# A two-block transformer on one core: the last expert pair adds into token-major PSUM, the final norm works per token tile, and the last eight weight chunks load in parts

## The chip, the core and the metric

The kernel runs on one core of one Trainium2 chip. A core has TensorE (matrix products, called PE in the rows; its weight loads are PEld), VectorE (DVE), ScalarE (ACT), GpSimd (POOL) and SyncE (SP), which issues most DMA transfers. The engines run their own instruction streams and meet at semaphores. Products land in PSUM, eight banks of 128 partitions x 512 float32; everything else lives in SBUF, in 128 partitions. The metric is the device time of one execution in microseconds (us). Lower is better.

## The reference, cut to what matters

Two transformer blocks on 512 tokens of width 1024, all in float32. Only the end of the second block is touched: the expert layer and the final norm.

```
D_MODEL = 1024; SEQ = 512; N_EXPERTS = 16; CAPACITY_FACTOR = 2; D_EXPERT = 2048

def rmsnorm(x, g):
    y = xf * lax.rsqrt(jnp.mean(xf * xf, axis=-1, keepdims=True) + EPS)
    return (y * g.astype(jnp.float32)).astype(x.dtype)

def expert_choice_ffn(h, w_router, w_gate, w_up, w_down):
    cap = max(1, CAPACITY_FACTOR * N // N_EXPERTS)            # 64
    aff = jax.nn.softmax(logits, axis=-1)
    top_w, top_idx = lax.top_k(jnp.swapaxes(aff, 1, 2), cap)
    xe = jax.vmap(lambda hb, ib: hb[ib])(h, top_idx)
    g = jnp.einsum('becd,edf->becf', xe, w_gate)
    u = jnp.einsum('becd,edf->becf', xe, w_up)
    y = jnp.einsum('becf,efd->becd', jax.nn.silu(g) * u, w_down)
    y = y * top_w[..., None].astype(y.dtype)
    return ...zeros((N, D)).at[ib.reshape(-1)].add(yb.reshape(-1, D))

    h2 = modulate_2(rmsnorm(x, norm2_g[l]), sh2, sc2)
    x = x + g2 * expert_choice_ffn(h2, ...)
    return rmsnorm(x, final_g)
```

Each of the 16 experts picks 64 tokens and multiplies them with three matrices of 8 MB each, 384 MB of weights in all.

## The kernel before

The first two thirds of the time (both blocks up to the router) are the same in both kernels. Then the experts follow in eight pairs, the loop `for it in range(PAIRS)` on every engine. The two experts of a pair share the 128 rows of the array: one takes PSUM partitions 0 to 63, the other 64 to 127.

A pair needs 24 weight chunks of 2 MB (`load`, L731): eight of the gate matrix, eight of up, eight of down. Each is [128 x 4096] float32, so a partition gets one run of 16 KB. There are eight chunk buffers (`eslots`: six tensors called weights, two pieces of the tensor arena). SyncE issues the chunks in order, each as soon as TensorE has counted the buffer's last user free (`chunk_free`). TensorE takes the chunks two by two, one per expert; such a step j has 16 matmuls of 512 columns.

Within a pair, TensorE does four steps of gate into banks 0 to 3, four steps of up into banks 4 to 7 (`widen`, L1301 and L1303), turns the hidden rows (`turn_hidden`, L1334), gathers the next pair's tokens (L1284) and does four steps of down into banks 4 and 5 (L1364 and L1367). ScalarE applies Silu (L1872), copies the turned rows (L1876) and, when the last down chunk is done, copies the two banks of y to SBUF (L1882). The next pair's first step is followed by `scatter` (L1316): eight matmuls, one for each 128 features, multiply y with a 0/weight matrix and give the pair's contribution feature-major, [128 features x 512 tokens]. VectorE multiplies each by the column g2 and adds it to the residual xT (L2506). So the scatter of a pair lies beside the next pair's weight stream.

After the last pair nothing follows that could cover it. There the order is: the two copies of y, the eight scatter matmuls, the eight adds; ScalarE squares each of the eight feature tiles (L1397) and TensorE sums over the features with 32 matmuls of one column (`norm_step`, L824); root and reciprocal of the [128 x 4] sums; VectorE has multiplied xT by the final weight in the meantime (L2531); TensorE turns 32 blocks of 128 x 128 back to token-major (L811), ScalarE and VectorE multiply by the reciprocal (L1391, L2537) and SyncE stores four tiles of 512 KB (L750).

The PSUM banks of the shared tiles are given out in order by `plan_banks`; the expert loop uses banks by number.

Of the kernel before, what the change touches and what calls it, by code (L numbers as in the profile page):

```python
# [25 lines left out]
ALU = mybir.AluOpType  # L26
# [114 lines left out]
def plan_banks():  # L141
# [129 lines left out]
    b.add("nf2", "A")  # L271
    for t in range(TT):
        for hh in range(2):
            b.add(("ot", t, hh), "AD"[hh])
# [3 lines left out]
def build_two_blocks(nc, x, c, ctx, c_ctx, w_mod, b_mod, norm1_w, w_in, ret_decay_f, ret_decay_b,  # L278
# [8 lines left out]
    with es:  # L287
# [42 lines left out]
        def slot(i, k):  # L330
# [11 lines left out]
            f_ready stored decay_exp stage2_in mod_summed mod_landed0 mod_landed1 mod_landed2""".split()  # L342
# [190 lines left out]
        LAST_BANK = 0 if banks.bank("nf2") >= 4 else 4  # L533
# [9 lines left out]
        norm_tags = ["n1", "nc", "n2", "n3", "nf1", "nc2", "n4", "nf2"]  # L543
# [4 lines left out]
        NTH_SQUARES = {2: 0, 3: 1, 4: 2, 6: 3, 7: 4}  # L548
# [122 lines left out]
        out_sb = at(0, TT, D)  # L671
# [17 lines left out]
        def _(sp):  # L689
# [53 lines left out]
            for it in range(PAIRS):  # L743
                for m in range(ESLOTS if it == 0 else 0, PAIR_CHUNKS):
                    sp.wait_ge(S["chunk_free"], LOOP_FREE + it * PAIR_CHUNKS + m - ESLOTS + 1)
                    load(it, m)
            for t in range(TT):
                for hh in range(2):
                    wait_freed(sp, ("ot", t, hh))
                sp.dma_start(out[0, t * P:(t + 1) * P, :], out_sb[:, t, :]).then_inc(S["stored"], 16)  # L750
            sp.wait_ge(S["stored"], 16 * TT)
# [3 lines left out]
        def _(pe):  # L755
# [563 lines left out]
            def weigh(it):  # L1319

                pe.wait_ge(S["hmt_ready"], FQ * it + 2)
                for t in range(TT):
                    pe.matmul(bank(1)[:, 0:2], sels[it % 2][:, t, :], aff[:, t, 2 * it:2 * it + 2],
                              start=(t == 0), stop=(t == TT - 1))
                for e in range(2):
                    pe.matmul(bank(0)[64 * e:64 * e + 64, :],
# [3 lines left out]
            def turn_hidden(it, n):  # L1330

                pe.wait_ge(S["hm_ready"], FQ * it + n + 1)
                for r in range(4):
                    last = pe.transpose(bank(n)[:, r * P:(r + 1) * P],  # L1334
                                        hmid[:, n * 512 + r:(n + 1) * 512:4], ident)
                last.then_inc(S["hmt_full"], 1)

# [3 lines left out]
            for it in range(PAIRS):  # L1341
                if it:
                    pe.wait_ge(S["wsel_ready"], it)
                for j in range(STEPS):
# [3 lines left out]
                    elif j == 0:  # L1348
                        gather(0, range(2, STEPS))
                if it:  # L1350
                    pe.wait_ge(S["x_added"], KT * it)
                for j in range(STEPS):
                    widen(it, j, 2 * STEPS, S["up_full"])
                for n in range(FQ):
# [3 lines left out]
                for j in range(STEPS):  # L1358
                    pe.wait_ge(S["hmt_ready"], FQ * it + j + 1)
                    m = 4 * STEPS + 2 * j  # L1360
                    wa, wb = expert_chunk(it, m, 4), expert_chunk(it, m + 1, 4)
                    for r in range(4):
                        for hh in range(2):
# [10 lines left out]
            pe.wait_ge(S["wsel_ready"], PAIRS)  # L1374
            scatter(PAIRS - 1, LAST_BANK)
            for k in range(KT):
# [1372 lines left out]
```

## Time and profile before

| | |
|---|---|
| time, median of 3 runs | 2497.77 us (2495.11 to 2498.15) |
| time of the profiled execution | 2498.93 us |
| its span in the trace | 2496.7 us |
| mean granted TensorE clock | 0.971 |
| busy share of PE, DVE, ACT, POOL | 93%, 36%, 25%, 6% |
| HBM read | 566.35 MB, 228 GB/s over the span |

Times in the rows are counted from the start of the span; the profiled execution's own time is 2.2 us longer than its span. A matmul in float32 appears in the trace as two records where it is a product and as one where it is a transpose. "x16" is a number of records, and records that follow each other overlap, so the distance from one start to the next is the cost of one, not its length. The granted clock has two levels: 1.00 is 2.4 GHz and 0.50 is 1.2 GHz.

### The profile page before, as it was taken

Reading aid. Unit: us, or ns where it says so; the run is one execution under the profiler, and the core shown is the slowest. Engines: PE = TensorE matmul, PEld = TensorE weight load, DVE = VectorE, ACT = ScalarE, POOL = GpSimd, SP = SyncE. Lnnn points to the kernel's source line nnn. Section 1 sums busy time; section 2 is a strip of 40 time slices with the busy share of each in tenths; the row PEclk is TensorE's granted clock in tenths of the full one; section 3 lists DMA queues with packets and bytes.
Section 4 is the critical chain, followed back from the end, with each engine's and each line's share of the span. In section 5 each row is a group of like instructions: output and inputs, shape, how many; then the busy total and the mean of one; then the engine's idle time right before and its main releaser. Section 6 shows DMA issues by size and latency. Waiting matters only on the chain.

```text
span 2496.7 us, 25781 instructions
## 1 busy us (share of the span) xinstructions
PE 2324.9 (93%) x11168; PEld 1520.2 (61%) x11168; DVE 897.7 (36%) x1178; ACT 621.6 (25%) x876; POOL 146.5 (6%) x140
## 2 busy tenths in 40 slices
PE   6999999999999999998999997988998889898988
PEld 4874878877888878786677885434343434242434
DVE  4937445455688334545632433010000000010102
ACT  5314333243334235415533221000000000000001
POOL 0221000110000011210000020000000000000000
PEclk8999999999999999999999998999999999999998
DMA  7220444344554331210012235999999999999994
GB/s 269 101 79 1 151 160 142 122 149 169 187 183 171 136 135 68 82 65 32 1 35 101 72 131 239 423 428 428 428 427 428 427 428 427 428 427 428 428 428 171
DMA packets 111190, 570.10 MB, mean 228 GB/s; under 512 B 5390, under 2 KB 28215, under 8 KB 86503
## 3 DMA queue, kind: packets, MB, share of 16 engines
q1 hardware_dynamic: 95200, 523.57, 51.9%
q0 software_dynamic: 7152, 27.99, 3.2%
q10 hardware_dynamic: 8727, 16.91, 1.9%
q8 instruction: 88, 1.44, 0.2%
q14 instruction: 23, 0.19, 0.0%
HBM read 566.35 MB, written 2.10 MB: 228 GB/s over the span
## 4 chain that ended last, share of the span: by engine, by line
PE 73%; DMA 19%; DVE 4%; ACT 2%; issue 1%; ACTq 0%; SPq 0%; POOL 0%; DVEq 0%; POOLq 0%
PE ps L772 42%; DMA arena<-in_w_exp_up 9%; PE ps L1301 8%; PE ps L1364 6%; DMA arena<-in_w_exp_gate 6%; PE ps L1284 3%; DMA weights<-in_w_exp_gate 2%; PE ps L1187 1%; PE ps L1205 1%; DMA arena<-in_w_exp_down 1%; PE ps L1145 1%; DMA weights<-in_w_up 1%; PE ps L1011 1%; PE ps L1316 1%; PE ps L1164 1%
## 5 line engine op out<-in xcount | busy, mean ns | idle before, releaser
L772 PE MATMUL ps<-weights_r 128*128 128x512 f32 (+1 forms) x2784 | 860.2, 389 | 12.1 <-DVE hT_r L1929 4.0
L772 PEld LDWEIGHTS ps<-weights_r 128*128 128x128 f32 x2784 | 521.0, 189 | 125.2 <-issue 18.7
L772 PE MATMUL ps<-hT_r,weights_r 128*128 128x512 f32 x1264 | 462.6, 390 | 0.0
L1301 PE MATMUL ps<-weights,arena 128*64 128x512 f32 x768 | 355.2, 620 | 61.0 <-DMA weights<-in_w_exp_up 47.7
L1303 PE MATMUL ps<-weights,arena 128*64 128x512 f32 x768 | 355.9, 621 | 0.0
L1301 PEld LDWEIGHTS ps<-weights,arena 128*64 128x64 f32 x768 | 106.2, 142 | 290.6 <-issue 288.6
L1910 DVE TENSOR_TENSOR weights_r<-weights,weights_r 128x4096 fp32r<-128x4096 f32 (+1 forms) x46 | 197.1, 4284 | 209.2 <-ACT weights_r L1447 207.4
L772 PEld LDWEIGHTS ps<-hT_r,weights_r 128*128 128x128 f32 x1264 | 238.3, 188 | 51.0 <-issue 2.2
L772 PE MATMUL ps<-arena_r,weights_r 128*128 128x512 f32 (+1 forms) x640 | 225.1, 388 | 0.0
L1447 ACT ACTIVATE weights_r<-weights 128x4096 fp32r<-128x4096 f32 (+1 forms) x46 | 161.6, 3514 | 214.8 <-PE ps L772 118.9
L2521 DVE TENSOR_TENSOR hT<-hT,ps 128x512 f32<-128x512 f32 x32 | 22.0, 688 | 461.8 <-PE ps L1303 461.8
L1364 PE MATMUL ps<-weights,hT 128*64 128x512 f32 x384 | 168.4, 594 | 2.3 <-DMA weights<-in_w_exp_down 2.3
L1367 PE MATMUL ps<-weights,hT 128*64 128x512 f32 x384 | 168.4, 594 | 0.0
L1301 PE MATMUL ps<-arena 128*64 128x512 f32 x256 | 119.3, 621 | 25.1 <-DMA arena<-in_w_exp_up 17.3
L772 PEld LDWEIGHTS ps<-arena_r,weights_r 128*128 128x128 f32 x640 | 120.6, 189 | 24.3
L1303 PE MATMUL ps<-arena 128*64 128x512 f32 x256 | 119.6, 622 | 0.0
L1364 PEld LDWEIGHTS ps<-weights,hT 128*64 128x64 f32 x384 | 51.2, 137 | 109.8 <-issue 108.8
L2506 DVE SCALAR_TENSOR_TENSOR xT<-ps,mod_cols,xT 128x512 f32<-128x512 f32 x64 | 48.0, 751 | 184.7 <-PE ps L1316 178.7
L1303 PEld LDWEIGHTS ps<-weights,arena 128*64 128x64 f32 x768 | 106.2, 142 | 0.0
L1301 PEld LDWEIGHTS ps<-arena 128*64 128x64 f32 x256 | 35.6, 143 | 101.4 <-issue 101.3
L1876 ACT ACTIVATE hT<-ps 128x512 f32<-128x512 f32 x32 | 16.5, 599 | 311.1 <-PE ps L1334 311.1
L1872 ACT ACTIVATE hT<-ps 128x512 f32<-128x512 f32 x32 | 19.1, 597 | 278.5 <-PE ps L1303 278.5
(294 smaller groups left out, 2531.6 us busy)
## 6 DMA issues: line engine op xcount, KB each, us to landing
weights<-in_w_exp_gate SPq DMA_DIRECT2D x48, 2048.0 KB, 23.1
weights<-in_w_exp_up SPq DMA_DIRECT2D x48, 2048.0 KB, 27.0
weights<-in_w_exp_down SPq DMA_DIRECT2D x48, 2048.0 KB, 27.1
weights<-in_w_in SPq DMA_DIRECT2D x18, 2048.0 KB, 8.3
arena<-in_w_exp_gate SPq DMA_DIRECT2D x16, 2048.0 KB, 27.1
arena<-in_w_exp_up SPq DMA_DIRECT2D x16, 2048.0 KB, 28.3
arena<-in_w_exp_down SPq DMA_DIRECT2D x16, 2048.0 KB, 28.5
weights<-in_w_up SPq DMA_DIRECT2D x22, 1024.0 KB, 7.7
```

The costliest lines, as they stand in the source:

```text
L772: last = pe.matmul(t, a if w_first else b, b if w_first else a, start=(k == 0 and n == 0), stop=(k == kt - 1 and n == len(pairs) - 1))
L1011: last = pe.matmul(t, v1[:, i, (2 * j + g) * DV:(2 * j + g + 1) * DV], probs[j % 2][g][:, i, :], start=(start and i == 0), stop=(not start ...
L1145: local = pe.matmul(ps[:, c:c + w], q2[o:o + 64, 2 * kv + p, n * P:(n + 1) * P], kdup[o:o + 64, kv, b0 * P:b1 * P], start=True, stop=False)
L1164: last = pe.matmul(ps[:, c + w + k0:c + w + k1], q2[o:o + 64, 2 * kv + p, n * P:(n + 1) * P], kcdup[o:o + 64, kv, k0:k1], start=True, stop ...
L1284: last = pe.matmul(bank(6, 2)[:, d * P:(d + 1) * P], h2_tok[:, t, 256 * j + r:256 * j + 256:2], sels[it % 2][:, t, :], start=(t == 0), sto ...
L1301: la = pe.matmul(bank(b0 + n)[0:64, :], xe[:, 2 * j + r, 0:64], wa[:, r, n * 512:(n + 1) * 512], start=start, stop=stop)
L1303: lb = pe.matmul(bank(b0 + n)[64:128, :], xe[:, 2 * j + r, 64:128], wb[:, r, n * 512:(n + 1) * 512], start=start, stop=stop)
L1364: la = pe.matmul(bank(4 + hh)[0:64, :], hmid_t[:, 4 * j + r, 0:64], wa[:, r, hh * 512:(hh + 1) * 512], start=(j + r == 0), stop=(j == STEP ...
L1367: lb = pe.matmul(bank(4 + hh)[64:128, :], hmid_t[:, 4 * j + r, 64:128], wb[:, r, hh * 512:(hh + 1) * 512], start=(j + r == 0), stop=(j == ...
L1447: A(slots_r[high_slot(i)][:, 0:n], slots[sl][:, 0:n], ACT.Copy).then_inc(S["high_ready"], 1)
L1910: ve.tensor_tensor(slots_r[sl][:, 0:n], slots[sl][:, 0:n], slots_r[high_slot(i)][:, 0:n].bitcast(F32), ALU.subtract).then_inc(S["low_ready ...
L2506: ve.scalar_tensor_tensor(xT[:, d, :], ps[:, b * 512:(b + 1) * 512], mod_cols2[:, 40 + d, 0:1], xT[:, d, :], ALU.mult, ALU.add).then_inc(S ...
```

## The change

In the last pair alone, the result is built token-major. While the last pair's weights stream, TensorE puts the residual of each of the four token tiles into two PSUM banks by multiplying xT with the identity (`turn_rest`); the last scatter then adds onto it, with the selection matrix as the stationary operand and y as the moving one. Since g2 can't be a per-partition column there, two rows (g2 and the final weight, each repeated over 128 partitions) are made by TensorE (`spread_rows`) and kept by ScalarE; y is multiplied by the g2 row when it leaves PSUM. The norm then is one squaring with a running sum per tile, a root, a reciprocal, and one VectorE operation per half tile that multiplies by both the reciprocal and the final weight. The last eight chunks load in halves (down steps 0 to 2) or quarters (step 3), with a semaphore of their own for each later part, and the down matmuls wait part by part.

```diff
+        TOKEN_BANKS = (0, 2, 6, 4)
+        g2_row, final_row = at(0, D), at(D, D)
+        out_sb = slots[0][:, :].rearrange("p (t d) -> p t d", t=TT)
+        squared = slots[1][:, :].rearrange("p (t d) -> p t d", t=TT)
@@ SyncE
+            for j in range(STEPS):
+                sp.wait_ge(S["chunk_free"], LOOP_FREE + PAIRS * PAIR_CHUNKS - 2 * ESLOTS + 2 * j + 2)
+                n = 4 if j == STEPS - 1 else 2
+                for i in range(n):
+                    for e in range(2):
+                        sl, w = 2 * j + e, SLOT // n
+                        src = w_exp_down_2[0, NE - 2 + e, 512 * j:512 * j + 512, :].rearrange(
+                            "(p r) n -> p (r n)", r=4)
+                        done = S[f"last{i}"] if n == 4 else S[f"late{j}"] if i else S[f"landed{sl}"]
+                        sp.dma_start(eslots[sl][:, i * w:(i + 1) * w], src[:, i * w:(i + 1) * w]).then_inc(done, 16)
+            for t in range(TT - 1):
+                sp.wait_ge(S["out_ready"], 2 * t + 2)
                 sp.dma_start(out[0, t * P:(t + 1) * P, :], out_sb[:, t, :]).then_inc(S["stored"], 16)
+            for hh in range(2):
+                sp.wait_ge(S["out_ready"], 2 * TT - 1 + hh)
+                sp.dma_start(out[0, L - P:L, hh * 512:(hh + 1) * 512], ...
@@ TensorE
+            def spread_rows(it):
+                pe.wait_ge(S["x_added"], KT * it)
+                for i, src in enumerate((mod_cols2[:, 40:48, 0], cols[:, 3, V1["final"]:V1["final"] + KT])):
+                    for k in range(KT):
+                        last = pe.matmul(bank(4 + 2 * i, 2)[:, k * P:(k + 1) * P],
+                                         src[:, k:k + 1].broadcast_to([P, P]), ident, start=True, stop=True)
+                    last.then_inc(S["rows_full"], 1)
+            def turn_rest(t):
+                for k in range(KT):
+                    pe.matmul(bank(TOKEN_BANKS[t], 2)[:, k * P:(k + 1) * P], xT[:, k, t * P:(t + 1) * P], ident,
+                              start=(k % 4 == 0), stop=False)
...
+                    if j == 2 and it == PAIRS - 1:
+                        spread_rows(it)
...
+                    if it == PAIRS - 1 and j in (1, 2):
+                        pe.wait_ge(S["silu_done"], FQ * PAIRS)
+                        turn_rest(j - 1)
...
+                        if in_parts:
+                            pe.wait_ge(S[f"last{r}"], 32)
+                        elif it == PAIRS - 1 and r == 2:
+                            pe.wait_ge(S[f"late{j}"], 32)
...
+                    if it == PAIRS - 1 and j == 2:
+                        pe.wait_ge(S["wsel_ready"], PAIRS)
+                        turn_rest(2)
-            scatter(PAIRS - 1, LAST_BANK)
-            for k in range(KT):
-                norm_step(7, "nf2", L, k)
             for t in range(TT):
+                if t == TT - 1:
+                    turn_rest(t)
                 for hh in range(2):
-                    turn(("ot", t, hh), [(k * P, hT[:, 4 * hh + k, t * P:(t + 1) * P]) for k in range(4)])
+                    pe.wait_ge(S["yg_ready"], hh + 1 if t == 0 else 2)
+                    pe.matmul(bank(TOKEN_BANKS[t] + hh), wsel_ts[(PAIRS - 1) % 2][:, t * P:(t + 1) * P],
+                              y_sb[:, hh * 512:(hh + 1) * 512], start=False, stop=True).then_inc(S["tok_full"], 1)
@@ ScalarE
+            A(small[:, 4:5], eps_col, ACT.Sqrt)
             for t in range(TT):
+                act_e.wait_ge(S["tok_full"], 2 * t + 2)
+                A(squared[:, t, :], ps[:, b * 512:(b + 2) * 512], ACT.Square,
+                  accum_out=tok_sums[:, t:t + 1]).then_inc(S["tok_squared"], 1)
+                act_e.wait_ge(S["tok_squared"], t + 1)
+                A(root[:, t:t + 1], tok_sums[:, t:t + 1], ACT.Sqrt, bias=eps_col, scale=1.0 / D).then_inc(
+                    S["tok_root"], 1)
@@ VectorE
+            for hh in range(2):
+                ve.tensor_tensor(y_sb[:, hh * 512:(hh + 1) * 512], bank(4 + hh), g2_row[:, hh * 512:(hh + 1) * 512],
+                                 ALU.mult).then_inc(S["yg_ready"], 1)
+            for t in range(TT):
+                ve.wait_ge(S["tok_root"], t + 1)
+                ve.reciprocal(recip[:, t:t + 1], root[:, t:t + 1]).then_inc(S["tok_recip"], 1)
+                ve.wait_ge(S["tok_recip"], t + 1)
+                for hh in range(2):
+                    c = slice(hh * 512, (hh + 1) * 512)
+                    ve.scalar_tensor_tensor(out_sb[:, t, c], bank(TOKEN_BANKS[t] + hh), recip[:, t:t + 1],
+                                            final_row[:, c], ALU.mult, ALU.mult).then_inc(S["out_ready"], 1)
```

In the last pair the turned hidden rows go to banks 4 to 7 and the last weight selection (`weigh`) to banks 6 and 7, since banks 0 to 3 then hold residuals; `weigh` therefore waits for all four copies of the turned rows, and the first down step for two.

TensorE's stream after the last matmul pairs of the last down step, in the kernel before (ps is PSUM, arena and hT are SBUF tensors; L1364 and L1367 are down, L1316 the scatter, L824 the sums, L811 the turns back):

```order
L1364 MATMUL ps<-arena,hT 64x512
L1367 MATMUL ps<-arena,hT 64x512
L1316 MATMUL ps<-arena 128x512 x8
L824 MATMUL ps<-mean_ones,arena 128x1 x32
L811 MATMUL ps<-cst,hT 128x128 x32
L287 UNCONDITIONAL_BRANCH
```

The same place in the changed kernel, with the waits (L1416 and L1419 are down, L1434 the scatter, L1372 `turn_rest`):

```order
L1416 MATMUL ps<-arena,hT 64x512 [waits last3]
L1419 MATMUL ps<-arena,hT 64x512
L1434 MATMUL ps<-arena 128x512 [waits yg_ready] x6
L1372 MATMUL ps<-cst,xT 128x128 x8
L1434 MATMUL ps<-arena 128x512 [waits yg_ready] x2
L283 UNCONDITIONAL_BRANCH
```

The sums and the turns back are gone; eight matmuls with the identity stand between the sixth and the seventh scatter matmul. Three more groups of eight stand earlier in the last pair: after up steps 1 and 2, and between down steps 2 and 3.

ScalarE's stream from the turned hidden rows of the last pair on, in the kernel before:

```order
L1876 ACTIVATE hT<-ps 128x512 x4
L1882 ACTIVATE arena<-ps 128x512 x2
L1417 ACT_TABLE_LOAD
L1417 ACTIVATE small<-small 128x1
L1397 ACTIVATE arena<-xT 128x512 x8
L1391 ACTIVATE small<-ps,small 128x4
L1391 ACTIVATE arena<-ps,small 128x512 x4
```

And in the changed kernel, where the last two rows stand four times:

```order
L1936 ACTIVATE hT<-ps 128x512 x4
L1945 ACT_TABLE_LOAD
L1945 ACTIVATE small<-small 128x1
L1949 ACTIVATE weights,small<-ps 128x1024
L1952 ACTIVATE small<-small 128x1
```

The copies of y have moved to VectorE, the table load stands ahead of the wait for the first token tile, and one squaring reads 1024 columns of PSUM at once.

SyncE's stream of the last down chunks and the stores, before:

```order
L731 DMA weights<-in_w_exp_down 128x4096 x6
L731 DMA arena<-in_w_exp_down 128x4096 x2
L750 DMA out<-arena 128x1024 x4
```

And after:

```order
L764 DMA weights<-in_w_exp_down 128x2048 x12
L764 DMA arena<-in_w_exp_down 128x1024 x8
L767 DMA out<-weights 128x1024 x3
L770 DMA out<-weights 128x512 x2
```

Eight loads have become twenty, and four stores five.

## Rows read from the trace of the kernel before

**Rows 1.** The page's strip: what the DMA engines moved, in 40 equal slices.

```profile
GB/s 269 101 79 1 151 160 142 122 149 169 187 183 171 136 135 68 82 65 32 1 35 101 72 131 239 423 428 428 428 427 428 427 428 427 428 427 428 428 428 171
```

**Rows 2.** The chain of waits: start, length, what; its last 70 us.

```profile
2429.53 29.80 DMA arena<-in_w_exp_down
2459.46 1.08 PE ps L1364
...
2468.09 1.09 ACT arena L1882 x2
2469.32 7.11 PE ps L1316 x16
2476.42 10.49 PE ps L824 x64
2486.91 5.03 PE ps L811 x32
```

**Rows 3.** Windows: stretch, length, busy of five engines, granted clock, DMA share, GB/s.

```profile
14.00:16.00 2.00, 2.00 (x16) 2.00 (x15) 0.84 (x2) 1.99 (x4) 0.00 (x0) 1.00 1.05 385
...
2200.00:2220.00 20.00, 20.00 (x100) 7.39 (x100) 3.16 (x9) 0.00 (x0) 0.00 (x0) 1.00 1.01 428
...
2457.00:2458.00 1.00, 0.00 (x0) 0.00 (x0) 0.00 (x0) 0.00 (x0) 0.00 (x0) 1.00 0.12 49
...
2480.00:2490.00 10.00, 10.00 (x49) 10.00 (x49) 1.30 (x3) 1.34 (x3) 0.00 (x0) 0.51 0.00 0
```

**Rows 4.** TensorE's timeline in the last pair; in brackets the idle time before.

```profile
2410.57 0.61 PE L1301 MATMUL ps<-weights,arena 128*64 128x512 f32 x1 [1.01 <-DMA weights<-in_w_exp_up]
...
2420.38 0.61 PE L1301 MATMUL ps<-arena 128*64 128x512 f32 x1 [2.71 <-DMA arena<-in_w_exp_up]
...
2431.22 0.64 PE L1364 MATMUL ps<-weights,hT 128*64 128x512 f32 x1
...
2439.94 0.61 PE L1364 MATMUL ps<-weights,hT 128*64 128x512 f32 x1 [1.63 <-DMA weights<-in_w_exp_down]
...
2446.96 1.05 PE L1323 MATMUL ps<-arena 128*128 128x2 f32 x8
...
2449.73 0.61 PE L1364 MATMUL ps<-weights,hT 128*64 128x512 f32 x1 [0.71 <-DMA weights<-in_w_exp_down]
...
2459.46 1.08 PE L1364 MATMUL ps<-arena,hT 128*64 128x512 f32 x1 [2.65 <-DMA arena<-in_w_exp_down]
...
2467.41 0.59 PE L1364 MATMUL ps<-arena,hT 128*64 128x512 f32 x1
```

**Rows 5.** The chain again: the last gather, 32 matmuls of 128 columns.

```profile
2312.28 7.54 PE ps L1284 x64
```

**Rows 6.** Groups by form on ScalarE and VectorE: busy, mean ns, idle before.

```profile
L1404 ACT ACTIVATE arena<-weights 128x1024 f32<-128x1024 f32 x8 | 8.4, 1048 | 0.0
L1404 ACT ACTIVATION_READ_ACCUMULATOR arena<-weights 128x1 f32 x8 | 1.5, 190 | 0.0
...
L2521 DVE TENSOR_TENSOR hT<-hT,ps 128x512 f32<-128x512 f32 x32 | 22.0, 688 | 461.8 <-PE ps L1303 461.8
```

**Rows 7.** ScalarE's and VectorE's timeline at the very end.

```profile
2469.19 1.28 ACT L1417 ACT_TABLE_LOAD   x1
...
2487.01 0.26 ACT L1391 ACTIVATE small<-ps,small 128x4 f32<-128x4 f32 x1 [9.13 <-PE ps L824]
...
2487.30 0.18 DVE L2534 RECIPROCAL small<-small 128x4 f32<-128x4 f32 x1 [6.93 <-ACT small L1391]
...
2490.21 2.50 DVE L2537 TENSOR_SCALAR arena<-ps,small 128x512 f32<-128x512 f32 x3 [0.64 <-PE ps L811]
```

**Rows 8.** DMA issues: count, KB of each, median us to landing.

```profile
weights<-in_w_in SPq DMA_DIRECT2D x18, 2048.0 KB, 8.3
...
out<-arena SPq DMA_DIRECT2D x4, 512.0 KB, 2.9
```

More of the change, by code:

```diff
@@ L670, in build_two_blocks, with turned_at, weighed_at @@
         hmid_t = hT[:, 4:8, :].rearrange("p a b -> p (a b)").rearrange("p (k n) -> p k n", k=16)
-        out_sb = at(0, TT, D)
+        def turned_at(it):
+            return 4 if it == PAIRS - 1 else 0
+        def weighed_at(it):
+            return 6 if it == PAIRS - 1 else 0
+        g2_row, final_row = at(0, D), at(D, D)
+        out_sb = slots[0][:, :].rearrange("p (t d) -> p t d", t=TT)
+        squared = slots[1][:, :].rearrange("p (t d) -> p t d", t=TT)
+        tok_sums = small[:, 48:52]
         decay = small[:, 8:24]
@@ L1358, in _ @@
                 for j in range(STEPS):
-                    pe.wait_ge(S["hmt_ready"], FQ * it + j + 1)
+                    pe.wait_ge(S["hmt_ready"], FQ * it + (max(j + 1, 2) if it == PAIRS - 1 else j + 1))
                     m = 4 * STEPS + 2 * j
-                    wa, wb = expert_chunk(it, m, 4), expert_chunk(it, m + 1, 4)
+                    in_parts = it == PAIRS - 1 and j == STEPS - 1
+                    if in_parts:
+                        wa, wb = (eslots[ESLOTS - 2 + e][:, :].rearrange("p (r n) -> p r n", r=4) for e in range(2))
+                    else:
+                        wa, wb = expert_chunk(it, m, 4), expert_chunk(it, m + 1, 4)
                     for r in range(4):
+                        if in_parts:
+                            pe.wait_ge(S[f"last{r}"], 32)
+                        elif it == PAIRS - 1 and r == 2:
+                            pe.wait_ge(S[f"late{j}"], 32)
                         for hh in range(2):
@@ L1866, in _ @@
                 free_before = LOOP_FREE + it * PAIR_CHUNKS
+                if it == PAIRS - 1:
+                    for i, dst in enumerate((g2_row, final_row)):
+                        act_e.wait_ge(S["rows_full"], i + 1)
+                        for hh in range(2):
+                            A(dst[:, hh * 512:(hh + 1) * 512], ps[:, (4 + 2 * i + hh) * 512:(5 + 2 * i + hh) * 512],
+                              ACT.Copy).then_inc(S["rows_kept"], 1)
                 for n in range(FQ):
```

70 lines of the change are left out of this document (29 added, 41 removed).

## The prediction, made before the changed kernel ran

> **What bounds the kernel now.** I read the page's strip first. From its 26th slice on the DMA engines move 427 or 428 GB/s in every slice, until the last, half empty one [rows 1]: the expert stage is bound by its weight stream. A matmul pair hidden or saved before the stream's end therefore buys nothing; what counts is what follows the last byte. The chain of waits says what that is [rows 2]. The last down chunk, issued at 2429.5, lands at 2459.4, and TensorE starts on it at 2459.46. From there to the end of the span, 2496.7, there are 37.2 us without a weight load: the last down step to 2468.0 (8.5 us), two copies of y to 2469.2, the scatter to 2476.4, the sums of squares to 2486.9, the turns back to 2491.9, then the last scaling and store. A single window, 2457 to 2458, shows the stream running out, at 49 GB/s [rows 3]: a few of the 16 engines end later than the others, and a chunk waits for the latest.
>
> In TensorE's timeline the reader is to see the waits in front of the steps [rows 4]. Up and down steps start 9.8 us apart (2410.57 to 2420.38, 2439.94 to 2449.73) since their 4.19 MB take that long; the work of a step, 16 pairs of records, is 6.9 us: `weigh` starts 7.0 us behind the step's first record (2439.94 to 2446.96), so a quarter of it is 1.72 and a pair 0.43. After an idle time of 1.63 us or less the first record lasts 0.61 to 0.64 us; the last down step, after 2.65 us of idle time, opens with 1.08 us, the lower clock level (1.2 GHz).
>
> **The change, part by part: up to the end of down.** The new matmuls with the identity, `turn_rest`, are products of 128 columns like the gather's, 32 of which took 7.54 us [rows 5]: 0.236 each, 1.9 us for a group of eight. `spread_rows` has 16, 3.8 us, in the gate phase. There and in up the 2.9 us between a step's work and the next landing cover them; the loads wait for chunks that are freed up to 2.5 us later, but the last of them has 29.8 us from issue to landing [rows 2], so the stream doesn't run dry. The first two groups even help: the group after up step 1 ends at about 2411.5 instead of the start at 2410.57, so step 2 ends near 2418.4, the second group near 2420.3, and step 3 starts at its landing, 2420.38, without the 2.71 us of idle time and without the low clock after it. That takes some 1.7 us off, and down starts at 2429.5 instead of 2431.22 [rows 4]. The wait for a second copy of turned rows costs nothing, since that copy is 0.5 us behind the first and TensorE still turns the last two.
>
> Then down, with halves landing 4.9 us ahead of the whole. Step 0 ends at 2436.4. The first half of step 1 is there at about 2435.2, the second at 2440.0; its two halves of work (3.4 us each) end at 2439.8 and, with a wait of 0.4, at 2443.7. `weigh` takes 2.0 us (2446.96 to 2449.0 before) to 2445.7. Step 2: first half at once, to 2449.1; the second lands at about 2450.3; done at 2453.7. The third group: 2455.6. Step 3 then has its first quarters already there and works through four times 1.72 us, to 2462.5. The other bound is the last quarter: landing at 2459.4 plus what the cutting costs (0.9, below), plus 1.72, is 2462.1. I take 2462.5, against 2468.0 before: a gain of 5.5 us, of which most is the parts' and the rest the higher clock.
>
> What cutting costs is not shown for 8 KB and 4 KB runs. The nearest rows bound it: at full DMA share 2 KB runs moved 385 GB/s and 16 KB runs 428 [rows 3]. One sixteenth of each, per packet, is 85.1 and 612.5 ns; a straight line through both has about 10 ns for a packet beside its bytes. The eight chunks have 1,024 packets of 16 KB; in parts they have 1,536 of 8 KB and 1,024 of 4 KB, which is 96 more for each engine, 0.9 us. The ends are 0 and the 2 KB rate for all 16.8 MB: 43.6 instead of 39.2 us, 4.4 us.
>
> The Trainium skill (DMA: Bandwidth & Descriptors, Why small descriptors are slow) gives a packet a fixed overhead of about three bus cycles. By its 850 MHz that would be an estimated 3.5 ns, 0.3 us in all; the row of the 2 KB runs speaks for more, and the sum goes by the row.
>
> **From the end of down to the end.** Before: 2468.0 to 2496.7, 28.7 us. Now: VectorE's product with the g2 row, PSUM to SBUF, 0.69 us [rows 6] and 0.07 for the semaphore; 0.15 to TensorE's start, as between 2469.17 and 2469.32 [rows 2]. The eight scatter matmuls cost what the old ones did, 7.11 / 8 = 0.89 each, 7.1 us; the fourth group, which stands between them, 1.9; 0.15 for the last to drain. TensorE ends 10.1 us after down. The second product of VectorE (0.69) lies beside the first matmul. The waits added here have behind them only the remaining matmuls of the same kind.
>
> For each token tile ScalarE squares 1024 columns with a sum, 1.05 + 0.19 [rows 6], and takes a root, 0.2; the reciprocal is 0.18 and two operations with the row are 0.83 apart [rows 7], 1.6 together. TensorE delivers a tile each 1.8 us, ScalarE needs 1.5 and VectorE 1.9 for one, and the fourth tile comes 3.7 us after the third. So three tiles lie beside TensorE's work and only the last one counts: 0.05 + 1.24 + 0.3 (root with its two hops) + 0.23 + 0.1 + 1.6 = 3.5 us. The table load (1.28 us, rows 7) now stands before the first wait, beside the down steps, at no cost; if that cover were gone it would cost nothing either way for the last tile. That root and squares need no further load is in the order of before, where eight squares and a root follow one load.
>
> The store: before, the last operation of VectorE ends at 2492.71 [rows 7] and the span at 2496.7, 4.0 us with four stores of 512 KB close together. Now the last is 256 KB and nearly alone. Its ends are 2.3 (the 2.9 of a 512 KB store [rows 8] less 0.6 for half the bytes) and 4.0; I take 3.3.
>
> The sum: 10.1 + 3.5 + 3.3 = 16.9 us instead of 28.7, a gain of 11.8. With the 5.5 that makes 17.3: span 2479.4. The profiled execution took 2498.93, so its like would take 2481.6; it lies 1.2 above the median of the runs shown. From 2497.77 the median comes to 2480.5.
>
> **The rivals.** *The stream ends later.* If parts move at the rate of 2 KB runs throughout, the last quarter lands at 2463.8 and down ends at 2465.6, 3.1 us later: 2483.6. For it: no row has runs of 4 or 8 KB from the expert matrices. Against: the packets stay longer than those that made 385 GB/s.
>
> *The lower clock in the tail.* TensorE waits 0.9 us after down, and before it works in bursts of 1.7 us. In the window 2480 to 2490 it had the 1.2 GHz level (0.51) though it was busy all the time, with matmuls of one column [rows 3]. If the final 9.0 us run at that level, they take 9.0 more: 2489.5; if only the first 3 us do, as at 2459.46, it is 1.6. Against: the old scatter, after 1.3 us of idle time, ran at full speed. The Trainium skill (TensorE: Matmul & The Clock Gate, HAM oscillation) warns of bursts that alternate with waits for transfers, where each burst starts at the low clock; by that rule the four quarters would cost up to 6.9 us. The trace agrees only for waits of 2.65 us.
>
> *Table loads in the tail.* If squaring PSUM with a sum and the root need different tables, each tile costs ScalarE 2 x 1.28 more, 4.1 us, and ScalarE becomes the bound from the first tile, 2.8 us after down: 2.8 + 4 x 4.1 + 1.9 + 3.3 = 24.4 instead of 16.9, so 2488.0.
>
> *Slower: the transfers' fixed cost.* A load of w_in (2 MB in 2 KB runs), issued when the queue has little in it, takes 8.3 us to landing [rows 8], of which 5.4 are its bytes at 385 GB/s; 2.9 are its own. If the stream had to pay this for each of the twelve additional loads one after the other, the last quarter would land 34.2 us later than now, at 2493.6, and down would end at 2495.3, 32.8 after the forecast's 2462.5: 2513.3. A store's own share (2.9 [rows 8] less 1.2 for 512 KB at 428 GB/s) is 1.7, and by that the time would be 2499.5. From 1.5 us for each load on it eats the whole gain. Against: loads queued 30 us deep run at 428 GB/s with no gap to be seen between them [rows 1, 3].
>
> The Trainium skill (DMA: Bandwidth & Descriptors, Bandwidth) advises transfers of at least 1 MiB for 75% of peak, and the same page has 2.0 us fixed for each; read so, 512 KB quarters would be the wrong size, and by its figure twelve loads would be an estimated 24 us.
>
> **How the numbers follow.** Forecast 0.66, its own range 2476.5 to 2484. Later stream 0.12 (2483.6), lower clock 0.13 (up to 2489.5), table loads 0.03 (2488.0), fixed cost 0.06, of which 0.03 at the load's price (2513.3) and 0.03 near the store's (2499.5). The lower end is the forecast with a free cut, a store of 2.3 us and the fastest of the shown runs (2.7 below the median): 2476. The upper end, 2488, takes in the later stream and most of the clock. What a measurement can't tell from no change is 0.2%, 5 us: faster 0.94 (all but the last), same 0.03 (the store's price), slower 0.03 (the load's).
>
> **What would show it.** In the new profile: TensorE's last down record ends near 2462.5; the second up wait and the last down wait are below 1 us; the DMA rate stays near 420 GB/s to 2450; eight scatter matmuls of 0.89 us with the identity group before the last two; no table load after 2440; three tiles stored before the fourth is squared; the span ends 16.9 us after down. I am wrong if the quarters' waits are seen on TensorE after 2461, if the granted clock is near 0.5 after down, or if ScalarE or VectorE finish a tile later than TensorE the next.

## The result and the profile after

The changed kernel takes 2480.07 us (median of 5 runs, 2477.48 to 2484.36), the kernel before 2498.15 us (5 runs, 2495.11 to 2500.42): a ratio of 0.9931, 95% interval 0.992 to 0.9942, so 14 to 20 us less. Forecast were 2480.5 us and 17.3 us less. The profiled execution took 2479.24 us with a span of 2477.0 us.

The chain of waits of the changed kernel from the second half of down step 2 on (start, length, what) answers to [rows 2]:

```profile
2421.87 27.08 DMA weights<-in_w_exp_down
2449.00 0.64 PE ps L1416
...
2452.65 1.98 PE ps L1372 x16
...
2461.22 0.42 PE ps L1416
2461.73 0.70 DVE arena L2596
2462.47 5.42 PE ps L1434 x12
2467.89 1.78 PE ps L1372 x16
2469.67 1.73 PE ps L1434 x4
2471.43 1.12 ACT weights L1949 x2
...
2473.11 0.75 DVE weights L2604
```

The last transfer on the chain is not the last of the stream: it is the second half of step 2, landing at 2449.0. After it everything is TensorE's own work until down ends at 2461.65. An identity group (the eight products of one token tile's residual with the identity, L1372) is among it. The sums and the turns back are gone.

TensorE's timeline in the last pair answers to [rows 4]:

```profile
2399.60 1.07 PE L1322 MATMUL ps<-weights,arena 128*64 128x512 f32 x1 [2.70 <-DMA weights<-in_w_exp_up]
...
2410.29 0.64 PE L1322 MATMUL ps<-weights,arena 128*64 128x512 f32 x1
...
2419.29 0.64 PE L1322 MATMUL ps<-arena 128*64 128x512 f32 x1
...
2428.42 0.64 PE L1416 MATMUL ps<-weights,hT 128*64 128x512 f32 x1
...
2449.00 0.64 PE L1416 MATMUL ps<-weights,hT 128*64 128x512 f32 x1 [0.79 <-DMA weights<-in_w_exp_down]
...
2454.57 0.64 PE L1416 MATMUL ps<-arena,hT 128*64 128x512 f32 x1
...
2461.06 0.59 PE L1419 MATMUL ps<-arena,hT 128*64 128x512 f32 x1
```

The place of an execution's expert stage in its span varies by a few us. All times below that begin with U are therefore counted from TensorE's start on the last pair's up step 1, which waits for its landing in every kernel: 2400.78 before, 2399.60 after. The span ends at U + 95.9 before and U + 77.4 after, 18.5 less. Down ends at U + 67.2 before, U + 62.05 after: 5.2 less (5.5 forecast). From there to the end, a stretch called the tail below, it is 28.7 and 15.35 us: 13.3 less (11.8 forecast). The remaining 1.2 us between the two spans lie ahead of U, where the time is set by work that is the same in both.

ScalarE's and VectorE's timeline, for [rows 6, 7], the last token tile and the table load:

```profile
2429.18 1.28 ACT L1945 ACT_TABLE_LOAD   x1
...
2471.43 1.02 ACT L1949 ACTIVATE weights<-ps 128x1024 f32<-128x1024 f32 x1 [2.06 <-PE ps L1434]
2472.35 0.20 ACT L1949 ACTIVATION_READ_ACCUMULATOR weights<-ps 128x1 f32 x1
2472.58 0.29 ACT L1952 ACTIVATE small<-small 128x1 f32<-128x1 f32 x1
```

```profile
2472.91 0.16 DVE L2600 RECIPROCAL small<-small 128x1 f32<-128x1 f32 x1 [1.90 <-ACT small L1952]
2473.11 1.41 DVE L2604 SCALAR_TENSOR_TENSOR weights<-ps,small,arena 128x512 f32<-128x512 f32 x2
```

VectorE ends at 2474.52, 3.1 us after TensorE's last record (3.5 forecast). The stores, for [rows 8]:

```profile
out<-weights SPq DMA_DIRECT2D x3, 512.0 KB, 2.6
out<-weights SPq DMA_DIRECT2D x2, 256.0 KB, 2.1
```

The windows (stretch, length, busy of five engines, granted clock, DMA share, GB/s) answer to [rows 3]:

```profile
2440.00:2445.00 5.00, 5.00 (x28) 1.98 (x26) 0.28 (x2) 0.00 (x0) 0.00 (x0) 1.00 1.02 415
2445.00:2450.00 5.00, 4.21 (x22) 1.29 (x20) 0.83 (x2) 0.00 (x0) 0.00 (x0) 1.00 1.02 408
...
2466.00:2470.00 4.00, 4.00 (x23) 2.79 (x22) 3.67 (x8) 2.82 (x6) 0.00 (x0) 1.00 0.32 131
```

With 8 KB and 4 KB runs the full queue moves 408 to 415 GB/s instead of 428. The tail's window has the full clock (1.00), where the kernel before had 0.51 in a window of its tail [rows 3].

### The profile page after: what moved, and what is told of

The parts are those of the page before. It is cut to its first block, busy times and chain, and to the rows that moved or that the text cites. A ratio compares the mean times of both kernels' runs of the same rounds, so it can differ in the third digit from the quotient of the medians.

```text
span 2477.0 us, 25779 instructions
## 1 busy us (share of the span) xinstructions
PE 2310.4 (93%) x11168; PEld 1507.6 (61%) x11168; DVE 892.9 (36%) x1171; ACT 619.6 (25%) x877; POOL 147.0 (6%) x140
## 4 chain that ended last, share of the span: by engine, by line
PE 73%; DMA 20%; DVE 4%; ACT 2%; issue 1%; SPq 0%; ACTq 0%; POOL 0%; DVEq 0%; POOLq 0%
PE ps L793 42%; PE ps L1322 8%; DMA arena<-in_w_exp_up 8%; PE ps L1416 6%; DMA arena<-in_w_exp_gate 5%; DMA weights<-in_w_exp_gate 3%; PE ps L1305 3%; PE ps L1208 1%; PE ps L1226 1%; DMA weights<-in_w_exp_up 1%; DMA weights<-in_w_exp_down 1%; PE ps L1166 1%; DMA weights<-in_w_up 1%; PE ps L1032 1%; PE ps L1337 1%
## 5 line engine op out<-in xcount | busy, mean ns | idle before, releaser
L793 PE MATMUL ps<-weights_r 128*128 128x512 f32 (+1 forms) x2784 | 859.7, 388 | 12.4 <-DVE hT_r L1995 4.0
L1416 PE MATMUL ps<-weights,hT 128*64 128x512 f32 x384 | 168.6, 594 | 0.8 <-DMA weights<-in_w_exp_down 0.8
L1419 PE MATMUL ps<-weights,hT 128*64 128x512 f32 x384 | 168.6, 594 | 0.0
L1416 PEld LDWEIGHTS ps<-weights,hT 128*64 128x64 f32 x384 | 51.1, 137 | 109.4 <-issue 105.9
L2573 DVE SCALAR_TENSOR_TENSOR xT<-ps,mod_cols,xT 128x512 f32<-128x512 f32 x56 | 42.0, 750 | 164.4 <-PE ps L1337 159.1
L1936 ACT ACTIVATE hT<-ps 128x512 f32<-128x512 f32 x32 | 16.5, 598 | 307.4 <-PE ps L1356 307.4
L2009 DVE SCALAR_TENSOR_TENSOR arena<-weights,sc_pad,arena 128x512 f32<-128x512 f32 x112 | 85.1, 760 | 4.0
```

The costliest lines, as they stand in the source:

```text
L793: last = pe.matmul(t, a if w_first else b, b if w_first else a, start=(k == 0 and n == 0), stop=(k == kt - 1 and n == len(pairs) - 1))
L1416: la = pe.matmul(bank(4 + hh)[0:64, :], hmid_t[:, 4 * j + r, 0:64], wa[:, r, hh * 512:(hh + 1) * 512], start=(j + r == 0), stop=(j == STEP ...
L1419: lb = pe.matmul(bank(4 + hh)[64:128, :], hmid_t[:, 4 * j + r, 64:128], wb[:, r, hh * 512:(hh + 1) * 512], start=(j + r == 0), stop=(j == ...
L2009: last = ve.scalar_tensor_tensor(acc, w[:, k, :], sc_pad[:, k, 0:1], acc, ALU.mult, ALU.add)
L2573: ve.scalar_tensor_tensor(xT[:, d, :], ps[:, b * 512:(b + 1) * 512], mod_cols2[:, 40 + d, 0:1], xT[:, d, :], ALU.mult, ALU.add).then_inc(S ...
```

## The experiments

Ratios are to the kernel before, with 95% intervals. The intervals are some 3 us wide each way, so differences among the variants are read from the traces, from U or from the end of down. Each variant has one trace.

**The changed kernel with whole loads.**

```diff
-                n = 4 if j == STEPS - 1 else 2      # parts of each chunk
+                load(it, m)                         # as before; the waits for parts are gone
```

> The changed kernel with the last eight chunks loaded whole again. My theory (the parts let TensorE work through the last down step while it lands): the last chunk lands near 2459.4, TensorE has no long wait before it, since an identity group stands there, and needs 6.9 us at the full clock: down ends at 2466.3 instead of 2461.7, the 15.3 us behind it stay, and the time is 4.5 us above the changed kernel's, ratio to before 0.995. Rival (the gain before the end of down is TensorE's earlier start and clock alone, the slowest DMA engine holds the last part back as much as the whole): 0 to 1 us above the changed kernel, ratio 0.993.

Measured: 0.9946 (0.9932 to 0.996), median 2484.24 us. Of its TensorE timeline:

```profile
2401.05 0.61 PE L1312 MATMUL ps<-weights,arena 128*64 128x512 f32 x1 [2.69 <-DMA weights<-in_w_exp_up]
...
2450.00 1.08 PE L1398 MATMUL ps<-weights,hT 128*64 128x512 f32 x1 [0.71 <-DMA weights<-in_w_exp_down]
...
2466.93 0.59 PE L1401 MATMUL ps<-arena,hT 128*64 128x512 f32 x1
```

Down ends at U + 66.5, 4.4 us later than with parts, and the span at U + 81.85, also 4.4 later; the tail is 15.4. So the parts are worth 4.4 us between these two traces, near the 4.5 expected; by the ratios it is 3.7. Two details are not as I expected. There is no wait before the last step: with the group before it TensorE gets there at U + 59.4, when the chunk is in. And step 2 opens at the low clock after only 0.71 us of idle time, which costs it 1.45 us (8.45 to the group behind it instead of 7.0). Such a stretch of records at 1.2 GHz is called a low stretch below. Without it TensorE would have waited for the chunk at U + 58.7, where it lands in the kernel before, and down would end near U + 65.8 by estimate. Some 0.7 of the 4.4 us is therefore the clock's. The rival (0 to 1 us) falls.

**Only the last step in quarters, steps 0 to 2 whole.**

```diff
-                n = 4 if j == STEPS - 1 else 2
+                n = 4 if j == STEPS - 1 else 1
```

> The changed kernel with down steps 0 to 2 loaded whole and only step 3 in quarters. The times are counted from TensorE's start on the last pair's up step 1, which has landed at the same point of the stream in every kernel. My theory (TensorE's own work is the bound from the second half of step 2 on): steps 1 and 2 start at their whole landings, 39.2 and 49.0 us, as in the kernel before, then 6.9 + 2.0 + 6.9 us: down ends at 64.7 instead of 62.0, and the time is 2.7 us above the changed kernel's. Rival (the last quarter's landing is the bound, and halves only add packets): down ends at 61 to 62, the time is equal or 0.5 us less.

Measured: 0.9944 (0.9929 to 0.9959), median 2484.41 us. Of its TensorE timeline:

```profile
2402.85 0.61 PE L1322 MATMUL ps<-weights,arena 128*64 128x512 f32 x1 [2.70 <-DMA weights<-in_w_exp_up]
...
2451.86 1.09 PE L1414 MATMUL ps<-weights,hT 128*64 128x512 f32 x1 [0.78 <-DMA weights<-in_w_exp_down]
...
2468.79 0.59 PE L1417 MATMUL ps<-arena,hT 128*64 128x512 f32 x1
```

Down ends at U + 66.5 and the span at U + 81.85, as with whole loads. I had U + 64.7; 1.45 us of the difference is the low clock after 2451.86, again behind a short wait (0.78 us). TensorE is the bound from step 2's landing on, with no wait before any quarter, so the rival falls: the halves are what let TensorE start early enough to meet the quarters. But the low stretch stands in both of these traces. Without it this one would end down near U + 65.1 and the one with whole loads near U + 65.8, both by estimate. So the quarters alone bring little, some 0.7 us; that they bring nothing is shown only at the low clock. Halves without quarters were not run. The last chunk's whole landing near U + 59 and 6.9 us of work would put down's end at about U + 66, so I expect, but it is not shown, that each needs the other.

**The kernel before with only the loads in parts.** The SyncE loop and the waits of the change, nothing else.

> The kernel before with only the loads in parts and the waits for them. My theory: down starts at 2431.2 as before, TensorE reaches the last quarter's work when that lands (about 2460), down ends at 2462.1 and the old tail of 28.7 us follows: 5.9 us less than before, ratio 0.9976. Rival (the parts pay only together with the identity groups that keep TensorE early and at the full clock): 2 us or less. Rival (twelve more loads have a fixed cost of 1.7 us each, one after the other): 14 us more than before.

Measured: 0.9977 (0.9968 to 0.9986), median 2492.72 us, 5.8 us less than before by the ratio. Of its TensorE timeline:

```profile
2404.16 1.09 PE L1311 MATMUL ps<-weights,arena 128*64 128x512 f32 x1 [2.52 <-DMA weights<-in_w_exp_up]
...
2463.48 0.64 PE L1382 MATMUL ps<-arena,hT 128*64 128x512 f32 x1 [0.55 <-DMA arena<-in_w_exp_down]
...
2466.72 7.11 PE L1326 MATMUL ps<-arena 128*128 128x512 f32 x16 [1.30 <-ACT arena L1900]
```

Of its chain of waits, the one-column sums, and the window about them:

```profile
2473.83 8.49 PE ps L834 x64
```

```profile
2473.00:2483.00 10.00, 10.00 (x70) 9.52 (x69) 4.84 (x11) 2.09 (x4) 0.00 (x0) 0.81 0.00 0
```

The window about the sums in the kernel before:

```profile
2476.00:2487.00 11.00, 11.00 (x66) 10.76 (x66) 4.27 (x10) 1.42 (x3) 0.00 (x0) 0.66 0.00 0
```

TensorE waits for the last quarter, which lands at U + 59.3, and down ends at U + 61.3, 6.0 us earlier than before and even 0.8 earlier than in the changed kernel. Neither rival holds. Here down starts at U + 30.4, as late as before, and ends no later for it. So the parts alone bring all of the gain before the end of down. Some 1.5 of the 6.0 us are the low stretch with which the last step opened before [rows 4]: 8.56 us, where a step takes 7.1.

The one-column sums took 8.49 us on the chain here and 10.49 before [rows 2], at a granted clock of 0.81 and 0.66 in these windows. A share of 0.66 over 11 us means 7.5 us at half speed, so 3.7 us lost; 0.81 over 10 us means 1.9 lost. The difference, 1.8, is nearly the 2.0 us between the two. By this estimate the sums would take some 6.7 us at the full clock, and 3.7 of the 13.3 us by which the change shortens the tail are the clock's: the changed tail has no such stretch.

The ratios of the two halves of the change can now be set side by side: the parts alone 5.8 us, all but the parts 13.5 us (whole loads, 0.9946), both together 17.2 us. They add up to 2 us more than the whole, which the intervals of 3 us don't tell apart from nothing.

**Identity groups of tiles 0 to 2 at the end.**

```diff
-                    if it == PAIRS - 1 and j in (1, 2):
-                        turn_rest(j - 1)
-                    if it == PAIRS - 1 and j == 2:
-                        turn_rest(2)
...
             for t in range(TT):
-                if t == TT - 1:
-                    turn_rest(t)
+                turn_rest(t)
```

> The changed kernel with the three identity groups of tiles 0 to 2 moved from the weight stream to the end, each ahead of its tile's scatter. My theory: the first one has 0.8 of its 2.0 us in TensorE's wait for VectorE, the others cost 2.0 each, so the tail is 5.1 us longer; down ends 0.8 us earlier, because its third group is gone, less what up step 3 loses by waiting 2.7 us and opening at 1.2 GHz: span about 4.3 us above the changed kernel, ratio to before 0.9948. Rival (the identity groups' main use is to keep the clock up): down ends 1.7 us later instead and the whole is 6.8 us above. Rival (TensorE has slack in the tail, ScalarE and VectorE set it): 1 us or less above.

Measured: 0.9942 (0.9929 to 0.9955), median 2483.02 us. Of its TensorE timeline:

```profile
2399.41 0.61 PE L1322 MATMUL ps<-weights,arena 128*64 128x512 f32 x1 [2.73 <-DMA weights<-in_w_exp_up]
...
2400.39 1.06 PE L1322 MATMUL ps<-weights,arena 128*64 128x512 f32 x1
...
2418.99 0.61 PE L1322 MATMUL ps<-arena 128*64 128x512 f32 x1 [2.70 <-DMA arena<-in_w_exp_up]
...
2458.73 0.64 PE L1413 MATMUL ps<-arena,hT 128*64 128x512 f32 x1 [0.56 <-DMA arena<-in_w_exp_down]
```

Down ends at U + 61.3, again 1.9 us behind the last quarter's landing at U + 59.3, 0.8 earlier than in the changed kernel; the tail is 19.8 us, 4.5 longer; the span ends 3.7 later (4.3 expected). Both rivals fall. The clock one falls by a surprise: up step 3, without a group ahead of it and after 2.70 us of idle time, runs at the full clock to its end here. Up step 1, after 2.73 us, opens with the same 0.61 and falls to the low clock 1.0 us later (2400.39).

**Weight selection in the gate phase, third group after down step 0.**

```diff
+                    if j == 1 and it == PAIRS - 1:      # gate step 1
+                        pe.wait_ge(S["x_added"], KT * it)
+                        weigh(it)
...
-                    if it == PAIRS - 1 and j == 2:      # down step 2
+                    if it == PAIRS - 1 and j == 0:      # down step 0
```

> The changed kernel with the last pair's weight selection done in its gate phase (beside the stream) and the third identity group behind down step 0 instead of step 2. My theory: the second half of down step 2 lands at 2449.0 whatever TensorE does, then 3.4 + 6.9 us of work follow without the group, and the last quarter's landing (about 2458.8) plus 1.7 becomes the bound: down ends near 2460.5, 1.2 us earlier, the tail is the same: 1.2 us below the changed kernel, 0.05%, which the times can't tell but the trace can. Rival (TensorE's work is not the bound at the end of down, the quarters are): down ends at 2461.7 as before, with waits of 1 us or more in front of the quarters.

Measured: 0.9928 (0.9915 to 0.9941), median 2479.38 us, not to be told from the change. Of its TensorE timeline:

```profile
2401.97 0.61 PE L1322 MATMUL ps<-weights,arena 128*64 128x512 f32 x1 [1.10 <-DMA weights<-in_w_exp_up]
...
2451.93 0.64 PE L1421 MATMUL ps<-weights,hT 128*64 128x512 f32 x1 [1.25 <-DMA weights<-in_w_exp_down]
...
2461.94 0.64 PE L1421 MATMUL ps<-arena,hT 128*64 128x512 f32 x1 [0.56 <-DMA arena<-in_w_exp_down]
```

Down ends at U + 61.9, 0.15 earlier. With the weight selection and the third group out of the way, TensorE now waits for quarters, 0.43 and 0.56 us, not the 1 us that the rival named: the last lands at U + 60.0 here. In the changed kernel itself the last quarter, issued at 2441.7, took 17.1 us to landing, so it was there at about U + 59.2, while TensorE came to it 0.8 us later. So the change sits near where both bounds meet. Why this variant's landing is 0.6 us later than in the others stays open.

**Gate and up in runs of 8 KB, all pairs, one transfer each.**

```diff
-                    src = ....rearrange("(p r) n -> p (r n)", r=2)
+                    src = ....rearrange("(r p) n -> p r n", r=2)
```

> The changed kernel with every gate and up chunk of all pairs loaded by one transfer as before, but with rows p and p+128 of the block in partition p instead of 2p and 2p+1, so that a partition gets two runs of 8 KB instead of one of 16 KB; the gather takes its columns to match. My theory (about 10 ns for each packet on each of the 16 DMA engines): 128 chunks have 128 more packets each, 1,024 more for an engine, 10 us more, stream at 421 instead of 428 GB/s in gate and up. Rival (a cut down to 8 KB costs nothing): 0. The Trainium skill's three bus cycles for a packet would be an estimated 3.6 us.

**The same runs by two transfers each.**

```diff
-                sp.dma_start(eslots[m % ESLOTS][:, :], src)
+                for w in (slice(0, SLOT // 2), slice(SLOT // 2, SLOT)):
+                    sp.dma_start(eslots[m % ESLOTS][:, w], src[:, w])
```

> The changed kernel with every gate and up chunk of all pairs loaded by two transfers of 1 MB instead of one of 2 MB, so the same packets of 8 KB as in the kernel with short runs, and 128 more transfers. My theory: 10 us more than the changed kernel, all of it the packets'; the transfers' own cost stays hidden in the queue, though SyncE is seen to be held in the issue. Rival (a transfer's fixed cost of 1.7 us or more shows when the queue can hold fewer of them): up to 128 x 1.7 = 218 us more, and DMA share below 0.95 somewhere.

Measured: 0.9956 (0.994 to 0.9973), median 2486.9 us, with one transfer, 0.9966 (0.9955 to 0.9978), median 2488.49 us, with two. Two TensorE waits that all kernels have, one in the second pair and up step 1 of the last, show the stream's length. First the changed kernel, then the one with short runs, then the one with two transfers:

```profile
1639.64 0.61 PE L1322 MATMUL ps<-weights,arena 128*64 128x512 f32 x1 [2.41 <-DMA weights<-in_w_exp_gate]
```

```profile
1639.31 0.61 PE L1325 MATMUL ps<-weights,arena 128*64 128x512 f32 x1 [2.65 <-DMA weights<-in_w_exp_gate]
...
2395.60 0.61 PE L1325 MATMUL ps<-weights,arena 128*64 128x512 f32 x1 [0.90 <-DMA weights<-in_w_exp_up]
...
2405.54 0.61 PE L1325 MATMUL ps<-weights,arena 128*64 128x512 f32 x1 [2.85 <-DMA weights<-in_w_exp_up]
```

```profile
1641.62 0.61 PE L1323 MATMUL ps<-weights,arena 128*64 128x512 f32 x1 [2.34 <-DMA weights<-in_w_exp_gate]
...
2408.07 0.61 PE L1323 MATMUL ps<-weights,arena 128*64 128x512 f32 x1 [2.86 <-DMA weights<-in_w_exp_up]
```

From the one to the other it is 760.0 us in the changed kernel (to 2399.60), 766.2 with short runs and 766.5 with two transfers. The stretch holds some 155 chunks (760 / 4.9), of which some 107 are gate or up, each with 8 more packets for an engine: 6.3 us over 856 packets is 7.3 ns for each. One step, 2395.60 to 2405.54, takes 9.94 us instead of 9.79, which is 9.4 ns. So a packet costs 7 to 10 ns beside its bytes; my 10 was the upper end, and the 10 us expected of the whole are 6.2 and 8.7 by the ratios. The twice as many transfers cost 0.3 us over 760 between these two traces, less than the 0.4 between the changed kernel and the one before: a transfer's fixed cost stays hidden, and the rival of 218 us falls. A packet for nothing falls too. The Trainium skill (DMA: Bandwidth & Descriptors, Why small descriptors are slow) has three bus cycles for a packet, an estimated 3.5 ns; the runs show two to three times that.

**Without the early table load.**

```diff
-            A(small[:, 4:5], eps_col, ACT.Sqrt)
             for t in range(TT):
```

> The changed kernel without the early dummy root that loads ScalarE's table. My theory: the load of 1.28 us falls behind the wait for the first token tile; tile 0 is done 1.3 us later, tiles 1 and 2 make it good in part, and tile 3, which comes 3.6 us behind tile 2, ends no later than now: tail within 0.3 us of 15.3. Rival (ScalarE has no slack up to tile 3): tail 16.6.

One run, 2476.89 us. The load appears once, between the first tile's squares and its root:

```profile
2463.05 0.19 ACT L1948 ACTIVATION_READ_ACCUMULATOR weights<-ps 128x1 f32 x1
2463.26 1.28 ACT L1951 ACT_TABLE_LOAD   x1
```

Down ends at 2459.29 and the span at 2474.6: a tail of 15.3 us. The pause that the identity group before the fourth tile gives ScalarE absorbs all of it. Squares and roots alternate over four tiles with this one load, so they share a table. Only the tail can be compared here: the third up landing came at U + 20.6, 1.0 us later than in the kernels above that wait for it (U + 19.6), and down ended at U + 63.0. Why is open.

**The last tile stored whole.**

```diff
-            for t in range(TT - 1):   # and two halves of the last
+            for t in range(TT):
```

> The changed kernel with the last token tile stored by one transfer of 512 KB instead of two of 256 KB. Theory: from VectorE's last operation to the end of the span 3.1 us instead of 2.5, since half the tile's bytes (0.6 us) no longer move ahead. Rival (the fixed part is all of it): 2.5 as now.

One run, 2479.34 us. VectorE ends at 2474.03 and the span at 2477.1: 3.1 us against 2.5, as expected. The halves are worth 0.6 us in this one pair of traces.

**The last tile squared in two halves.**

```diff
+                if t == TT - 1:
+                    for hh in range(2):
+                        act_e.wait_ge(S["tok_full"], 2 * t + 1 + hh)
+                        A(squared[:, t, ...], ps[:, ...], ACT.Square, accum_out=...)
...
```

> The changed kernel with the last token tile squared in two halves: the first while TensorE does the second half's scatter matmul; VectorE makes the first sum into the root's bias. Theory (ScalarE's 1.12 us of squaring stand alone on the path for the last tile): the half that is left takes 0.6 + 0.2, so the last reciprocal comes 0.3 to 0.5 us earlier and the tail is 14.9 to 15.0 us instead of 15.3. Rival (the additional read of the accumulator and the wait for VectorE, which is busy with tile 2, take it back): 15.3 or more.

Measured: 0.9913 (0.9896 to 0.993), median 2477.51 us. Of ScalarE's timeline:

```profile
2475.43 0.60 ACT L1951 ACTIVATE weights<-ps 128x512 f32<-128x512 f32 x1 [0.17 <-PE ps L1434]
2475.92 0.19 ACT L1951 ACTIVATION_READ_ACCUMULATOR weights<-ps 128x1 f32 x1
```

Down ends at 2465.65 and the span at 2480.6: a tail of 14.95 us, 0.4 less, as expected. Only the tail is shorter in the trace: the third up landing came at U + 20.95, 1.4 us later than in those kernels, for a reason that stays open, and the span ends at U + 78.3, 0.9 later than the change's. In the times its interval overlaps the change's, so that the whole kernel is faster than the change is not shown.

## Why the prediction was right, step by step

- **What counts is what follows the stream.** Right. The stream is as long as before, 759.6 and 760.0 us between the two common waits, and the gain lies behind U.
- **The end of down, 5.5 us.** 5.2 measured. The forecast had TensorE's own work as the bound, at 2462.5, and the last quarter's bound 0.4 ahead of it. Measured, the work is the bound by 0.8 us (down ends at U + 62.05 against U + 61.3 in the two kernels that wait for the quarter). That the early start would add its share to the parts' does not hold: with the parts alone down ended 6.0 us earlier, though it started no earlier than before. With the parts in place an early start ends in the wait for the quarter, and the third group takes 0.8 us back.
- **The clock's 1.7 us.** The amount appeared, the reason given for it is wrong. Down started at U + 28.8 instead of U + 30.4. But the kernel without the early groups also reached its turned rows at U + 26.6, as the changed one did at U + 26.7: after 2.70 us of idle time its step 3 kept 2.4 GHz. The step that failed is the reading that a first record of 0.61 us, after an idle time of 1.63 us or less, means the full clock, and that 2.65 us of idle time costs it. The rows themselves [rows 4] have a first record of 0.61 after 2.71 us, at 2420.38. The clock fell behind it, in the middle of the step:

```profile
2421.84 1.06 PE L1301 MATMUL ps<-arena 128*64 128x512 f32 x1
```

In the whole trace of the kernel before, 20 weight steps follow an idle time of 2.65 to 2.80 us. Eleven of them have a low stretch, which begins up to 1.5 us after their start; five of the eleven open with 0.61. Nine have none. Of 17 steps after 0.7 to 1.7 us of idle time none has one, but two variants fell to the low clock after 0.71 and 0.78 us. So long waits make a low stretch likely, the idle time in front of a step does not decide it, and what does is open. A low stretch makes a step 1.4 to 1.7 us longer. That the early groups removed one here was, by the variant without them, partly luck; the prediction's sentence that the trace agrees only for waits of 2.65 us goes by the same first records.
- **Cost of cutting, 0.9 us.** Two halves' step 2 lands at U + 49.4 instead of U + 48.95, 0.45 for six chunks; the last quarter at U + 59.3 instead of U + 58.7, 0.6. The term was 0.3 too large by these, while one variant's last quarter landed at U + 60.0, 1.3 later than the whole chunk before.
- **The tail, 16.9 us.** 15.35 measured, each term a little smaller: TensorE's part 9.7 instead of 10.1, the last tile 3.1 instead of 3.5 (two VectorE operations take 1.41, not 1.6), the store 2.5 instead of 3.3. The store was the largest miss: I took 3.3 out of the range from 2.3 to 4.0, and the lower end was nearly right. A last store of 512 KB took 3.1, so even that is below the 4.0 of before, where four stores stood close together; how much the other stores cost was not separated.
- **Rivals.** *Later stream:* not seen, the rate is 408 and not 385 GB/s. *Low clock in the tail:* not seen; from the end of down to TensorE's last record the granted clock is 1.00 in the changed kernel and in all its variants. *Table loads:* one only. *Fixed cost:* excluded for quarters by the parts alone, which made the kernel before faster, and for 1 MB by the two transfers.

The terms miss in opposite directions: the gain before the end of down was 0.3 less than forecast, the gain in the tail 1.5 more. The median came out at 2480.07 against 2480.5, closer than the terms. That is luck within what five runs can tell.

## What to carry to other kernels

A last weight step can be worked through while it lands only if TensorE gets there in time: cut the steps ahead of it too. Work that would stand in the tail goes into the waits ahead of the last steps: three identity groups there cost the end of down 0.8 us, and at the end they cost the tail 4.5. Where nothing follows, the layout in which the output leaves counts: adding in place in PSUM in token order did away with 10.5 us of one-column sums and 5.0 us of turns back for 1.8 us of identity products on the chain, and made the tail 13.3 us shorter, of which an estimated 3.7 are the low clock that the sums had. Whether a wait will cost the clock can't be told from its length, nor from the first record behind it: it showed up to 1.5 us on. Take 1.4 to 1.7 us for one low stretch into the range.

## What the runs showed of the hardware

SyncE was held in issuing when many packets stood in the queue. The eight quarter loads of the changed kernel (durations min/median/max in ns):

```profile
L764 SPq DMA_DIRECT2D arena<-in_w_exp_down x8: 328/2132/6292, 2426.4 to 2441.7; - x8
```

The two whole loads in their place before:

```profile
L731 SPq DMA_DIRECT2D arena<-in_w_exp_down x2: 328/380/431, 2429.2 to 2429.5; - x2
```

With short runs a single transfer of 2 MB was also held, 2.14 us at 2384.35, so the number of transfers alone does not explain it. At their landing times of 25 to 30 us and 421 GB/s some 1,300 to 1,600 packets of 8 KB stand in the queue (estimated from these), against 780 of 16 KB before. It cost nothing there: over 500 us (1800 to 2300) the DMA share was 1.01, as without short runs. Exactly what is counted is open.

The last two quarters of the changed kernel, issued at 2439.6 and 2441.7, took 12.4 and 17.1 us to landing. Meanwhile the stream ran out, at 229 GB/s from 2450 to 2455 and 39 from 2455 to 2460. That is not the parts' doing: the kernel before has 285 and 79 GB/s in the same windows, at a DMA share of 0.67 and 0.18. Those bytes, 1.8 MB, would be through 4.3 us after 2450 at 428 GB/s, but the last chunk landed at 2459.3. So by estimate some 5 us of the wait for the last chunk, before and after, is a stream that a few DMA engines finish later than the rest. The change leaves that as it is; why the engines end unevenly is open.
